# Dilated attention in 24 equal two-step units, decay rows by DMA, and an unnormalised differential map

## The reference

```python
proj = xn @ w_in            # q, k, v of all mixers, and the gates
# mixer A: dilated window attention, groups of dilation 1, 4, 16, 6 heads of 64 each
s = einsum(qb, kw) / sqrt(Dh);  s = where(mask, s, -1e30)
mx = max(s);  p = exp(s - mx);  den = sum(p)
o = (p / den) @ vw;  lse = mx + log(den)
alpha = softmax(stack(lse))                 # over the 3 groups
o_a = sum(alpha * outs)
# mixer B: mLSTM over (4 heads, 2 directions), decay weights exp(logD - m_t)
# mixer C: differential attention, 4 heads
p = softmax(q @ k / sqrt(dk));  a = p[0] - lam * p[1];  o = a @ v
o_c = rms_norm(o, c_hn_g) * (1 - lam_init)
# merge
mixed = gates0 * y_a + gates1 * y_b + gates2 * y_c
x = x + mixed @ w_out
x = x + (silu(hg) * hu) @ w_ffn_out
```

## Time and profile before

| | before |
|---|---|
| median of 3 runs | 3615.83 us (3612.37 to 3620.4) |
| the profiled execution | 3621.54 us |
| its span | 3619.9 us |
| granted TensorE clock, mean | 0.952 |
| busy: PE, DVE, ACT, POOL | 90%, 44%, 32%, 13% |

### The profile page before, as it was taken

How to read it: one execution, slowest core, us unless ns; L and a number is a source line. 1 busy time by engine, 2 the same in 40 slices (tenths; PEclk the granted TensorE clock), 3 DMA queues, 4 the chain that set the end, 5 groups by cost and what they waited for, 6 DMA issues and landing times. The chain is left out here.

```text
span 3619.9 us, 45917 instructions
## 1 busy us (share of the span) xinstructions
PE 3258.0 (90%) x17716; PEld 2952.0 (82%) x17716; DVE 1596.1 (44%) x3321; ACT 1164.2 (32%) x2456; POOL 483.8 (13%) x854
## 2 busy tenths in 40 slices
PE   6899988998876999999978899879988779999998
PEld 6789876887766799999878898768877668999997
DVE  5345256453345334434453442564434453344434
ACT  4334423554422221111143334235553222121111
POOL 0111311211233000000001114112112220000000
PEclk9899998999997999999988999999999979999999
DMA  3434433333455122112043344333335551222111
GB/s 128 132 98 132 129 126 98 112 91 99 145 141 162 47 70 70 54 50 70 30 131 96 104 132 126 125 101 105 94 100 156 131 169 35 66 70 70 54 50 64
DMA packets 273050, 358.60 MB, mean 99 GB/s; under 512 B 27128, under 2 KB 209592, under 8 KB 272856
## 3 DMA queue, kind: packets, MB, share of 16 engines
q1 hardware_dynamic: 214520, 182.59, 17.0%
q0 software_dynamic: 58336, 173.45, 15.5%
HBM read 261.27 MB, written 94.69 MB: 98 GB/s over the span
## 5 line engine op out<-in xcount | busy, mean ns | idle before, releaser
L1648 PE MATMUL ps<-wh,xh 128*128 128x384 f32 (+1 forms) x1536 | 579.3, 377 | 19.3 <-DVE wl L1259 6.6
L1649 PE MATMUL ps<-wl,xh 128*128 128x384 f32 (+1 forms) x1536 | 563.8, 367 | 0.0
L1650 PE MATMUL ps<-wh,xl 128*128 128x384 f32 (+1 forms) x1536 | 563.7, 367 | 0.0
L1259 DVE TENSOR_TENSOR wl<-wraw,wh 128x1024 fp32r<-128x1024 f32 (+2 forms) x210 | 232.3, 1111 | 429.0 <-ACT wh L1000 429.0
L1648 PE MATMUL ps<-xh,wh 128*128 128x384 f32 (+1 forms) x1056 | 374.0, 354 | 38.2 <-DVE ol L1345 14.9
L1718 PE MATMUL ps<-xh,wh 128*128 128x384 f32 x1408 | 361.1, 337 | 20.1 <-DVE arena L1635 15.3
L1649 PE MATMUL ps<-xl,wh 128*128 128x384 f32 (+1 forms) x1056 | 360.3, 341 | 0.0
L1650 PE MATMUL ps<-xh,wl 128*128 128x384 f32 (+1 forms) x1056 | 360.2, 341 | 0.0
L1718 PE MATMUL ps<-xl,wh 128*128 128x384 f32 x1408 | 359.0, 336 | 0.0
L1718 PE MATMUL ps<-xh,wl 128*128 128x384 f32 x1408 | 358.8, 335 | 0.0
L1648 PEld LDWEIGHTS ps<-wh,xh 128*128 128x128 f32 x1536 | 299.0, 195 | 55.1 <-DVE ol L1345 7.1
(11 more groups left out here) (211 smaller groups left out, 5315.8 us busy)
## 6 DMA issues: line engine op xcount, KB each, us to landing
wraw<-in_w_in SPq DMA_DIRECT2D x96, 512.0 KB, 4.1
wraw<-in_w_ffn_in SPq DMA_DIRECT2D x88, 512.0 KB, 4.0
wraw<-in_w_in SPq DMA_DIRECT2D x72, 384.0 KB, 3.4
wraw<-in_w_ffn_out SPq DMA_DIRECT2D x44, 512.0 KB, 3.4
qkv_a<-stage POOLq DMA_DIRECT2D x108, 192.0 KB, 2.2
gate_t<-stage POOLq DMA_DIRECT2D x96, 192.0 KB, 2.2
stage<-gate_t POOLq DMA_DIRECT2D x96, 192.0 KB, 2.8
mix_t<-stage POOLq DMA_DIRECT2D x64, 192.0 KB, 3.8
```

Source lines behind the costliest of these rows:

```text
L1259: dve.tensor_tensor(wl[:, half, j, 0:w], wraw[:, n % RAW, 0:w], wh[:, half, j, 0:w].bitcast(F32), ALU.subtract).then_inc(w_lo, 1)
L1648: pe.matmul(out, ah, bh, start=first, stop=False)
L1649: pe.matmul(out, ah, bl, start=False, stop=False)
L1650: return pe.matmul(out, al, bh, start=False, stop=last)
```

## The change

**Mixer A.** A tile of group 0 becomes two units of three heads, so that there are 24 units with 6 x 128 columns of probabilities each, in place of 18. The list of steps is written anew: `a_out(u-1)` and `a_score(u)` in one place, `a_turn(u)` after `GAP_A` of dense work, and behind it the fold of the next prep as soon as no unit needs its slot of `a_qk`. `a_p` and `a_pt` are double buffered, the three PSUM places are fixed. The maximum is taken of negated, scaled scores (as a minimum), so the small scalings go, and ACT waits for each head. A store and the loads behind it come with the last unit of a tile.

```diff
+            for t in range(n):
+                if g == 0:
+                    units += [(g, s, t, [base + t, base + t + 1], range(3 * i, 3 * i + 3)) for i in range(2)]
+                else:
+                    units.append((g, s, t, [base + t], range(A_H)))
+    last = [max(u for u, x in enumerate(units) if p in x[3]) for p in range(len(preps))]
...
+    def loads(done):
+
+        nonlocal loaded
+        while loaded < len(preps) and (loaded < 3 or last[loaded - 3] < done):
             order.append((("a_load", loaded), 0))
             loaded += 1
...
-            order += [(("a_fold", folded), GAP_A[2]), (("a_turn", u), 0)]
-            folded += 1
-        else:
-            order.append((("a_turn", u), GAP_A[2]))
-        order.append((("a_out", u), GAP_A[3]))
...
+            order.append((("a_out", u - 1), gap))
+            gap = 0
+        loads(u)
+        while folded <= unit[3][-1]:
+            fold(2 * GAP_A if folded == 0 else GAP_A)
+            gap = GAP_A
+        order += [(("a_score", u), gap), (("a_turn", u), GAP_A)]
+        if folded < loaded and (folded < 3 or last[folded - 3] <= u):
+            fold(0)
+    order.append((("a_out", len(units) - 1), GAP_A))
+    return preps, units, last, order
...
                     def store_unit(u):
-                        g, s, t, _ = UNITS[u]
+                        i = A_TILE[u]
+                        g, s, t = A_TILES[i]
+                        if UNITS[u][4][-1] != A_H - 1:
+                            return
                         pool.wait_ge(a_ov, u + 1)
...
-                            nk = len(UNITS[u][3])
-                            for h in range(A_H):
-                                if h % (A_H // 2) == 0:
-                                    act.wait_ge(a_mx, 2 * u + 1 + h // (A_H // 2))
-                                pr = a_p[:, h * nk * P:(h + 1) * nk * P]
-                                ins = act.activation(pr, pr, ACT.Exp, bias=unit_s[:, h:h + 1], scale=HD ** -0.5,
-                                                     accum_out=a_o[:, u % 2, A_W + A_H + h:A_W + A_H + h + 1])
+                            nk, heads, i = len(UNITS[u][3]), UNITS[u][4], A_TILE[u] % 2
+                            for j, h in enumerate(heads):
+                                act.wait_ge(a_mx, A_MAX[u] + j + 1)
+                                pr = a_p[:, u % 2, j * nk * P:(j + 1) * nk * P]
+                                ins = act.activation(pr, pr, ACT.Exp, bias=a_o[:, i, A_W + h:A_W + h + 1], scale=-1.0,
+                                                     accum_out=a_o[:, i, A_W + A_H + h:A_W + A_H + h + 1])
...
-                            for h in range(A_H):
-                                if h == A_H // 2:
-                                    chain.wait()
-                                    dve.tensor_scalar(unit_s[:, 0:h], a_o[:, u % 2, A_W:A_W + h], -HD ** -0.5, None,
-                                                      ALU.mult).then_inc(a_mx, 1)
...
+                            for j, h in enumerate(heads):
+                                dve.tensor_tensor_reduce(
+                                    a_p[:, u % 2, j * nk * P:(j + 1) * nk * P].rearrange("p (k n) -> p k n", k=nk),
+                                    score_bank(u, h).rearrange("p (k n) -> p k n", k=nk), mk, -HD ** -0.5, 3e38, ALU.add,
+                                    ALU.min, a_o[:, i % 2, A_W + h:A_W + h + 1]).then_inc(a_mx, 1)
```

```diff
+
+                        s, h = B_UNITS[u]
+                        t0, n = SEQS[s]
+                        if u >= 2:
+                            pool.wait_ge(b_dec, u - 1)
+                        pool.dma_start(b_nb[:, u % 2, :, 0:n * P], nmx_d[:, h, t0 * P:(t0 + n) * P].partition_broadcast(P)
+                                       ).then_inc(b_nbin[u % 2], 16)
 
...
                         elif kind == "b_columns":
+                            pool.wait_ge(bg_scan, 4)
+                            pool.dma_start(nmx_d.rearrange("d h n -> h d n"), nmx[0:4, :, :]).then_inc(nmx_out, 16)
                             pool.wait_ge(bg_cols, 2)
+                            pool.wait_ge(nmx_out, 16)
+                            load_decay(0)
+                            load_decay(1)
...
+                                load_decay(step[1] + 1)
                         elif kind == "b_out":
...
-                        elif kind == "b_decay":
-                            u = step[1]
-                            s, h = B_UNITS[u]
-                            t0, n = SEQS[s]
-                            if u:
-                                pe.wait_ge(b_h, u)
-                            for d in range(2):
-                                mm = pe.matmul(side[:, 512 * (2 + d):512 * (2 + d) + n * P],
-                                               ident[0:4, h:h + 1].to_broadcast([4, P]),
-                                               nmx[0:4, d, t0 * P:(t0 + n) * P], start=True, stop=True)
-                            mm.then_inc(b_bc, 1)
...
-                            pe.wait_ge(b_dec, u + 1)
```

```diff
-                            chain.link(dve.tensor_reduce(unit_s[:, 32:34], side[:, 0:1024].rearrange(
-                                "p (m n) -> p m n", m=2)[:, :, 0:n * P], AX_X, ALU.max))
-                            dve.tensor_scalar(unit_s[:, 34:36], unit_s[:, 32:34], -HD ** -0.5, None, ALU.mult
-                                              ).then_inc(c_mx, 1)
+                            k = c_s[:, u % 4, :]
+                            dve.tensor_reduce(k[:, 0:2], side[:, 0:1024].rearrange("p (m n) -> p m n", m=2)[:, :, 0:n * P],
+                                              AX_X, ALU.max, negate=True).then_inc(c_mx, 1)
                             dve.wait_ge(c_ex, 2 * (u + 1))
-                            chain.link(dve.reciprocal(unit_s[:, 38:40], unit_s[:, 36:38]))
-                            chain.link(dve.tensor_tensor(unit_s[:, 39:40], unit_s[:, 39:40], lam[:, 0:1], ALU.mult))
-                            e0, e1 = c_e[:, 0, 0:n * P], c_e[:, 1, 0:n * P]
-                            chain.link(dve.tensor_scalar(e1, e1, unit_s[:, 39:40], None, ALU.mult))
-                            dve.scalar_tensor_tensor(e0, e0, unit_s[:, 38:39], e1, ALU.mult, ALU.subtract
-                                                     ).then_inc(c_a, 1)
+                            chain.link(dve.reciprocal(k[:, 4:6], k[:, 2:4]))
+                            chain.link(dve.scalar_tensor_tensor(k[:, 6:7], k[:, 5:6], lam[:, 0:1], k[:, 2:3], ALU.mult,
+                                                                ALU.mult))
+
+                            dve.scalar_tensor_tensor(c_e[:, 0, 0:n * P], c_e[:, 1, 0:n * P], k[:, 6:7],
+                                                     c_e[:, 0, 0:n * P], ALU.mult, ALU.subtract).then_inc(c_a, 1)
...
-                            dve.tensor_copy(c_o[:, h * P:(h + 1) * P], side[:, 1536:1536 + P]).then_inc(c_ov, 1)
+                            dve.tensor_scalar(c_o[:, h * P:(h + 1) * P], side[:, 1536:1536 + P], c_s[:, u % 4, 4:5], -1.0,
+                                              ALU.mult, ALU.mult).then_inc(c_ov, 1)
```

More of the change, by code:

```diff
@@ L151, in prep_list, with fold @@
-    return preps, units, order
-PREPS, UNITS, A_ORDER = prep_list()
-LAST_USE = [1 + max(u for u, x in enumerate(UNITS) if p in x[3]) for p in range(len(PREPS))]
+    def fold(gap):
+        nonlocal folded
+        order.append((("a_fold", folded), gap))
+        folded += 1
+    for u, unit in enumerate(units):
+        gap = GAP_A
+        if u:
+            order.append((("a_out", u - 1), gap))
[3 more added lines that the diff above has]
+            fold(2 * GAP_A if folded == 0 else GAP_A)
+            gap = GAP_A
+        order += [(("a_score", u), gap), (("a_turn", u), GAP_A)]
+        if folded < loaded and (folded < 3 or last[folded - 3] <= u):
+            fold(0)
@@ new lines, in prep_list @@
+    order.append((("a_out", len(units) - 1), GAP_A))
+    return preps, units, last, order
+PREPS, UNITS, LAST_UNIT, A_ORDER = prep_list()
+LAST_USE = [1 + u for u in LAST_UNIT]
+A_TILES = [(g, s, t) for g, s, t, _, heads in UNITS if heads[-1] == A_H - 1]
+A_TILE = [A_TILES.index(x[:3]) for x in UNITS]
+A_KINDS = [k[0] for k, _ in A_ORDER]
+FOLDS_BEFORE = [A_KINDS[:i].count("a_fold") for i, k in enumerate(A_KINDS) if k == "a_score"]
+SCORES_BEFORE = [A_KINDS[:i].count("a_score") for i, k in enumerate(A_KINDS) if k == "a_fold"]
@@ L159, in token_rows @@
+A_MAX = [sum(len(x[4]) for x in UNITS[:u]) for u in range(len(UNITS) + 1)]
 def token_rows(g, s, t, halo):
@@ L418, in build @@
         gates_b = dram("gates_b", (16, TOK))
+        nmx_d = dram("nmx_d", (2, B_H, TOK))
         gate_t = dram("gate_t", (3, D, TOK))
@@ L445, in build @@
         unit_s = sb("unit_s", [P, 64])
+        c_s = sb("c_s", [P, 4, 8])
         arena_floats = 10400
@@ L542, in build @@
             sem(x) for x in ("bg_in", "bg_abs", "bg_ln", "bg_scan", "bg_col", "bg_cols"))
```

(28 more changed lines are left out.)

134 lines of the change are left out of this document (55 added, 79 removed).

## The result

The changed kernel takes 3651.2 us (median of 4 runs, 3647.8 to 3663.2) against 3618.1 us for the kernel before on the same chip: 1.0092 of its time, with a 95% interval of 1.0074 to 1.011. It is **33 us slower**; the forecast was 14 us slower, with a range that ended at 3646. The profiled execution after has a span of 3661.6 us (the slowest of the four), so its profile shows 41.7 us over the earlier trace rows's execution where the medians show 33.

What follows compares the result with a forecast made beforehand. PE, busy 90% of the span in a fixed order, was taken as the bound. Terms of +21.6 (A), +2.2 (B) and -10 (C) gave +13.8 us over the median 3615.83: 3629.6 us, range 3604 to 3646.

Steps and rivals of the forecast that it cites:

- The turns: In mixer A, PE's waits for exponentials: 6.2 us a layer after the change in place of some 13.
- The folds: In mixer A, PE's waits for loads from qkv_a at six folds: 20.7 us a layer after the change.
- What PE does in A: In mixer A, as many scores as before, half a score at 0.9 us; part A in all +10.8 us a layer.
- 1.6 us a drop: On PE, a wait of 2 us or more lowers the clock to 0.59 over the next 4 us: 1.6 us more.
- B, the first b_qk: In mixer B, conv_in delayed by the nmx_d write and loads: 3.7 us wait plus 1.6 clock in layer 1, 6.1 in layer 2.
- B, the long units: In mixer B, removed broadcasts gain 0.6 us each in units 4 and 7, nothing in 5 and 6.
- the short units: In mixer B, removed broadcasts gain 1.06 us in each of units 0 to 2, and 0.2 in unit 3.
- its own rule of two us: On PE, a wait of 2 us or more costs more than itself through a lower clock; waits of 0.7 us don't.
- C: In part C, less DVE work shortens the chain from score to mixed map: -5 us a layer, -10 in all.
- slower by more: Rival: late folds hold back later stages, landings near 6 us, B's conv load behind a 3.8 us write: 3648 us, chance 0.19.

Runs made afterwards that it cites:

- e5: The changed kernel with each fold of mixer A placed no sooner than the first unit that needs it: 3618.9 us, 0.9996 of before.
- e3: The changed kernel with the wait for the nmx_d write and the first decay loads moved behind conv_in and b_vo: 3634.7 us, 1.0047 of before.
- e2: The changed kernel with the removed broadcast matmuls put back on PE, unread, in the long units of B: 3639.4 us, 1.0053 of before.
- e9: The kernel before with part B alone, decay loads behind conv_in and b_vo, unread matmuls back in the long units: 3609.6 us, 0.9968 of before.
- e8: The kernel before with part C of the change alone: 3611.7 us, 0.9977 of before.
- e7: The kernel before with part B of the change alone: 3632.7 us, 1.004 of before.
- e1: The changed kernel with mixer B as before (broadcast by matmul, no nmx_d), A and C changed: 3640.0 us, 1.0053 of before.
- e4: The changed kernel with four slots of a_in in place of three and a_pt single: 3577.5 us, 0.9882 of before.
- e10: The changed kernel with four slots of a_in and mixer B as before: 3612.0 us, 0.9983 of before.
- e12: The changed kernel with four slots of a_in, folds no sooner than needed, and decay loads behind conv_in: 3560.8 us, 0.9837 of before.

## Why the prediction was wrong, by its own steps

**The turns: right in direction, near in size by luck.** Forecast 6.2 us a layer behind the change; L1801 waited 11.1 us in both layers, 5.5 a layer. But 2.85 of it is one turn of a later group that the forecast did not have, and behind a weight split the turn waits 0.17 us, not 0.65.

**The folds: right.** Folds 3, 4, 7, 8, 9 were to wait 3.5, 5.15, 2.55, 4.5, 4.4 us; they waited 3.8, 4.1, 2.45, 4.3, 3.6. (Its sum of the six is 20.8, written as 20.7.) The landing of the earlier trace rows held: the same loads took 3.7 to 5.7 us after, median 4.2. e5 shows that the place of the folds makes the waits. By the figure of the Trainium skill (DMA: Bandwidth & Descriptors, Anatomy of one DMA) the waits would be 2.3, 2.9, 1.8, 1.5 and 0.7. This trace does not show that.

**What PE does in A: two steps that were wrong, and luck in the sum.** The forecast took 1.6 us a drop from the earlier trace rows, where the wait was 2.11 us, and used it for waits of up to 5; the five folds lost 2.2 us each (11.1 in all for 8.0), and the turn of 2.85 us one more drop. And it put the work at nothing ("the scores are as many as before", half a score at 0.9 us): they are as many, but half a score takes 1.16 us, 3.7 us a layer. Over the stretch of A in layer 1 PE is thus busy 8.5 us longer, 3.7 by scores and the rest by clock, where the forecast had 1.6 for both. The idle time grew by 3.5 us where it had 9.1: after, PE stood idle 24.5 us for 26.9 forecast, and before, 21.0 us for 17.8, mostly since it left out the folds' waits on issue (L1751, 5.7 us in both layers), which the new order no longer has. The errors nearly cancel (12.0 measured, 10.8 forecast). A alone is +27.8 by its median, 6 over the forecast.

**B, the first b_qk: right.** POOL waited 2.86 us for the write (2.9 taken), and the first b_qk 3.3 and 3.1 us. The delay at the next b_qk is +5.0 and +5.2 us with the gain of unit 0 in it, some 6.2 without (5.3 and 6.1 forecast). e3 confirms the place. Of the short units, 1 and 2 gained 1.3 us each and unit 3 gained 0.25 (1.06 and 0.2 forecast).

**B, the long units: the step that failed.** The forecast said of them "there less work means more wait", saw the 1.12 us wait, and put their gain at 0.2 to 0.6 us or nothing. It did not add the removed 2 us to the wait and hold the sum, 3.1 us, against its own rule of two us above. By that rule alone (sharper than the runs bear out, as the last section shows) the out step would have lost its clock. It did: 3.05 to 3.53 us of wait in three units of four, out steps of 7.51, 6.38 and 7.65 us for 4.7, +8.5 and +9.9 us a layer (7.5 and 7.0 to the first score of C) against -1.2 forecast. The longer wait by itself costs little, as it stands where the removed matmuls stood; the loss is in the out steps, 64.9 us for 49.9 in both layers. e2 and e9 show that it is the idle time and not the source of the rows. With this term at +7 to +10 a layer the sum would have been 3646 to 3652.

**C: right.** -8.4 against -10. In the short sequence the turns wait 0.18 us in place of 0.51. In the long one part of the gain is given back at the transposes of rows of o_tok (waits for them 21.3 us in e8, 17.5 before). That POOL's chain of mix stores sets the pace there is what the forecast argued; no run tests it.

**The rivals.** The one called slower by more had the size (3648) with the wrong cause: landings of 6 us and a late write. The landings were as forecast.

What stays open: the size of B. The medians give +12.6 (e7) and +11.2 (e1), the profiled executions of e7 and of the kernel before +14.4, and the aligned profile of the changed kernel +24 to the first fold of C, +19 to its first score. And e4 moves slots and places together; how much of its 74 us is the place of B's steps was not measured apart, beyond e10 and e12.

## What to carry to other kernels

Work taken off an engine that then waits is not merely without gain: if the longer wait lowers the clock, the work behind it pays, here 15 us in two layers. So add what is removed to the wait that stands behind it, and price the sum again. A transfer that is issued one step ahead of its use is a wait to be looked up in landing times; move the use back or give the ring one more slot before anything else. When a step list is merged by weights, a small edit moves everything behind it, and that can be worth more (e4) than the edit. And half a step is not half the time: price it from its own instructions, here pairs of heads of which three heads make only one.

## What the runs showed of the hardware

- The granted clock stayed at 1.00 behind waits of 1.1 to 1.4 us of PE (out steps before and in e2). Behind waits of 2 to 3.2 us it went either way, for equal waits too. Before, it fell behind 2.11 us at 152.08 and 174.96 and not at 278.93; it fell behind 2.97 us in layer 1 (212.11) and not in the same step of layer 2 (2014.22). In e2 it stayed at 1.00 behind the 3.16 us wait of the first b_qk in layer 1. It fell behind every fold and long out step of the changed kernel that had waited 3.4 us or more. Of before:

```profile
278.90:284.90 6.00, 5.97 (x41) 5.97 (x41) 3.89 (x9) 2.66 (x6) 0.56 (x1) 1.00 0.14 40
212.00:218.00 6.00, 5.89 (x29) 5.89 (x30) 3.02 (x8) 1.96 (x5) 0.54 (x1) 0.72 0.10 36
2014.20:2020.20 6.00, 5.98 (x41) 5.98 (x41) 3.02 (x8) 2.05 (x5) 0.54 (x1) 1.00 0.10 36
```

- The time lost did not follow the wait: 1.6 us behind 2.11, 2.7 behind 3.77, 1.7 behind 4.13, and in the out steps 1.6 behind 3.53 and 2.9 behind 3.51 and 3.05. So a price for one drop is right on the average only.
- Two matmuls of 64 partitions each that read different halves started together (1.71 us for 24), where one half had no partner they did not (1.16 us for 12).
- A write of 24 KB from four partitions to DRAM landed 2.9 and 3.0 us behind its issue (L973, the two layers).
- Exponentials of 128 columns took 388 ns with their input in SBUF (L1183 after) and 355 with it in PSUM (L1146 before), by the groups of ACT by form.

The Trainium skill, VectorE: DVE Perf Modes, section The TRN2 errata — SBUF-src ops pay a fixed extra latency per instruction, says that ScalarE has a longer fixed latency for a source in SBUF (224 cycles) than in PSUM (172). The trace agrees in sign, and nearly in size: 52 cycles at the 1.2 GHz of that table are 43 ns, by an estimate, and the rows show 33. A long unit has six such readings on ACT (L1183 and L1185, 128 to 384 columns), 17 to 37 ns longer each than before, 0.18 us together. That is part of the 0.3 us left in e2; the rest is not shown.
